# A weight ring of three slots instead of four, and half an expert chunk fetched early into the freed memory

## The reference, cut to what matters

```python
proj = h @ w_in[l]                       # first block: 1024 x 15368
ym = hm @ w_proj_m[l]; ya = ha @ w_proj_a[l]
x = x + gate[:, None] * (y @ w_out[l])
# second block: w_in, w_out again, and then
xs = jax.vmap(lambda hb, ib: hb[ib])(h, idx)
a = jnp.einsum('becd,edf->becf', xs, w_gate)
u = jnp.einsum('becd,edf->becf', xs, w_up)
y = jnp.einsum('becf,efd->becd', jax.nn.silu(a) * u, w_down) * gate[..., None]
```

## Time and profile before

| | |
|---|---|
| median of 3 runs | 1555.35 us (1554.5 to 1555.72) |
| profiled execution, its own time | 1554.04 us |
| span of that execution | 1552.2 us |
| TensorE busy | 1198.4 us (77%) |
| VectorE busy | 614.4 us (40%) |
| ScalarE busy | 425.8 us (27%) |
| HBM read | 548.36 MB |
| rate of the transfers, slices 17 to 39 of 40 | 390 to 432 GB/s |
| dense loads at L520 | 93 of 1 MiB, 5.4 us from issue to landing in the median |

### The profile page before, as it was taken

One profiled execution on the slowest core, in us unless ns is written; L12 is line 12 of the kernel. 1 busy time (PEld: TensorE's weight loads), 2 busy tenths in 40 slices (PEclk: granted clock), 3 DMA queues, 4 the chain that ended last, 5 costly groups with the idle time before them and its releaser, 6 DMA issues.

```text
span 1552.2 us, 18204 instructions
## 1 busy us (share of the span) xinstructions
PE 1198.4 (77%) x7368; PEld 696.7 (45%) x7368; DVE 614.4 (40%) x1041; ACT 425.8 (27%) x644; POOL 36.9 (2%) x62
## 2 busy tenths in 40 slices
PE   7999999999999999976666665665655665665665
PEld 5888977887887899721111111111111111111112
DVE  3786789889777876511011011011011011110111
ACT  3665357786554674300000000000000000000001
POOL 0000000010001000000000000000000000000000
PEclk9999999999999999988777787787878877777788
DMA  9876877687756666999999999999999999999996
GB/s 362 284 263 216 308 245 246 231 307 235 273 183 209 215 220 245 390 432 430 430 432 430 430 431 432 430 432 432 432 429 431 432 430 431 431 430 430 432 432 276
DMA packets 78323, 550.62 MB, mean 355 GB/s; under 512 B 5032, under 2 KB 5320, under 8 KB 61856
## 3 DMA queue, kind: packets, MB, share of 16 engines
q1 hardware_dynamic: 75168, 541.08, 86.2%
q0 software_dynamic: 2784, 8.08, 1.7%
q10 hardware_dynamic: 288, 0.30, 0.1%
HBM read 548.36 MB, written 1.61 MB: 354 GB/s over the span
## 4 chain that ended last, share of the span: by engine, by line
PE 43%; DMA 36%; DVE 12%; ACT 4%; issue 3%; SPq 0%; DVEq 0%; ACTq 0%; POOL 0%
PE ps L610 41%; DMA b<-in_w_down 34%; DVE b L1535 6%; ACT b L1171 3%; PE ps L614 3%; DVE b L1552 2%; DVE b L2265 1%; ACT b L1173 1%; DVE b L2206 1%; DMA b<-in_w_in 1%; DMA b<-in_w_ada 1%; DVE b L2212 1%; DVE b L1545 0%; ACT L1171 0%; DVE b L1566 0%
## 5 line engine op out<-in xcount | busy, mean ns | idle before, releaser
L610 PE MATMUL ps<-b,b 128*32 128x512 f32 (+7 forms) x6922 | 1130.3, 541 | 300.0 <-DMA b<-in_w_up 117.3
L610 PEld LDWEIGHTS ps<-b,b 128*32 128x32 f32 (+2 forms) x6922 | 640.9, 159 | 750.5 <-issue 456.5
L1171 ACT ACTIVATE b<-ps 128x512 f32<-128x512 f32 (+3 forms) x165 | 92.2, 559 | 868.7 <-PE ps L610 560.7
L1535 DVE TENSOR_TENSOR b<-b,b 128x1024 fp32r<-128x1024 f32 (+5 forms) x254 | 277.1, 1091 | 98.1 <-ACT b L1171 78.9
L1171 ACT ACTIVATE b<-b 128x1024 fp32r<-128x1024 f32 (+6 forms) x219 | 219.1, 1001 | 213.9 <-PE ps L610 161.2
L2255 DVE TENSOR_TENSOR b<-b,ps 128x512 f32<-128x512 f32 x16 | 11.0, 687 | 395.6 <-issue 382.3
L2265 DVE TENSOR_TENSOR b<-b,ps 128x1024 f32<-128x1024 f32 x28 | 34.2, 1222 | 304.3 <-PE ps L610 304.3
L614 PE MATMUL ps<-b,b 128*128 128x128 f32 (+1 forms) x360 | 69.7, 322 | 38.4 <-DVE b L1566 23.5
L614 PEld LDWEIGHTS ps<-b,b 128*128 128x128 f32 (+1 forms) x360 | 45.8, 168 | 88.9 <-DVE b L1566 36.4
L1552 DVE SCALAR_TENSOR_TENSOR b<-b,b,b 128x512 f32<-128x512 f32 (+3 forms) x50 | 63.2, 1263 | 4.3 <-ACT b L1171 0.5
L1535 DVE TENSOR_TENSOR b<-ps,b 128x512 f32<-128x512 f32 (+8 forms) x69 | 37.6, 545 | 26.5 <-PE ps L610 14.9
(11 more groups left out here) (59 smaller groups left out, 201.0 us busy)
## 6 DMA issues: line engine op xcount, KB each, us to landing
b<-in_w_up SPq DMA_DIRECT2D x30, 4096.0 KB, 43.2
b<-in_w_gate SPq DMA_DIRECT2D x29, 4096.0 KB, 43.0
b<-in_w_down SPq DMA_DIRECT2D x29, 4096.0 KB, 38.5
b<-in_w_in SPq DMA_DIRECT2D x73, 1024.0 KB, 5.6
b<-in_w_ada SPq DMA_DIRECT2D x28, 1024.0 KB, 5.5
b<-in_w_gate SPq DMA_DIRECT2D x6, 2048.0 KB, 9.0
b<-in_w_down SPq DMA_DIRECT2D x5, 2048.0 KB, 13.0
b<-in_w_ada SPq DMA_DIRECT2D x16, 512.0 KB, 11.4
```

The lines of the kernel that those rows point to most:

```text
L610: return e.matmul(o, lhsT, rhs, start=start, stop=stop, skip_group_check=True)
L1171: e.activation(o, i, f, bias=bias, scale=scale).then_inc(mark[0], 1)
L1535: e.tensor_tensor(o, a, b, op).then_inc(mark[0], 1)
```

## The change

`RING` becomes 3, so that load i goes to slot i % 3 and waits for the load three places before it. The memory of the fourth slot (24 to 32 KB of the ring's area) is the upper half of the place of chunk 7. This half (1 MiB, columns 2048 to 4095 of the chunk) is now fetched right behind chunk 0, before load 92. The lower half, which lies in slot 2, is fetched where the whole chunk was. The waits for chunk 7 count both halves. The sizes and the number of bytes stay, and there is one transfer more.

```diff
--- before.py
+++ after.py
@@ -167,7 +167,7 @@
     ADA_STEP[_step] = [ADA_STEP[_step], NADA_PE + _a] if _step in ADA_STEP else NADA_PE + _a
 ADA_AT = {step: a if isinstance(a, list) else [a] for step, a in ADA_STEP.items()}
 ADA_SUM = {(13, 0): "R3", (17, 0): "R2", (26, 0): "R4"}
-RING = 4
+RING = 3
 LOADS = []
 
 
@@ -268,6 +268,8 @@
 
 E_PAIR_FREE = (5, 9, 11, 12, 14)
 
+IN_HALVES = E_ORDER.index("ring2")
+
 SCRATCH = 1024
 
 
@@ -476,7 +478,7 @@
         def expert_weight(n):
 
             if n < E_FIRST:
-                return EW[n], (S(f"ew{n}"), 16) if n < NCH else (S(f"ada0_{n % 2}_0"), 48)
+                return EW[n], (S(f"ew{n}"), 32 if n == IN_HALVES else 16) if n < NCH else (S(f"ada0_{n % 2}_0"), 48)
             m, g = (n - E_FIRST) // 2, n % 2
             return EP[m % E_PAIRS][:, g * 4096:(g + 1) * 4096], (S(f"ew{m % E_PAIRS}"), 16 * (m // E_PAIRS + 2))
 
@@ -531,6 +533,11 @@
                 ada0(1, k)
                 if k == 0:
                     ring_load(2)
+            def half_load(n, h):
+                o, (landed_, _) = expert_weight(n)
+                hs = slice(h * 2048, (h + 1) * 2048)
+                e.dma_start(o[:, hs], chunk_src(n)[:, hs]).then_inc(landed_, 16)
+
             def expert_load(n):
                 o, (landed_, _) = expert_weight(n)
                 e.dma_start(o, chunk_src(n)).then_inc(landed_, 16)
@@ -538,6 +545,7 @@
             for i in range(3, len(LOADS) - 1):
                 if LOADS[i] == ("w", SLACK):
                     expert_load(0)
+                    half_load(IN_HALVES, 1)
                 if LOADS[i] == ("w", CONTEXT_DONE):
 
                     e.wait_ge(S("v_x"), 2 * NT)
@@ -560,7 +568,7 @@
             e.wait_ge(S("v_ry"), 1)
             expert_load(6)
             e.wait_ge(S("v_lo"), NHALF - 4)
-            expert_load(7)
+            half_load(IN_HALVES, 0)
             e.wait_ge(S("v_lo"), NHALF)
             expert_load(8)
             e.wait_ge(*full("WP0b"))
@@ -1137,7 +1145,7 @@
 
 
             def last_part(q):
-                e.wait_ge(S(f"ew{E_PAIRS + q}"), 32)
+                e.wait_ge(S(f"ew{E_PAIRS + q}"), 48 if E_PAIRS + q == IN_HALVES else 32)
                 for b in (2 * (q % 2), 2 * (q % 2) + 1):
                     ins = down_last(w, 3, b, q // 2)
                 ins.then_inc(S("p_use"), 1)
```

## The result

The changed kernel took a median of **1574.55 us** (1572.18 to 1574.99, four runs), the kernel before 1555.53 us (1554.5 to 1559.75, four runs): a ratio of **1.012**, 95% interval 1.0104 to 1.0135. The forecast was 1562.0, and slower: the direction was right, and the delay was 19.0 us where the prediction's terms add up to 6.8. The profiled execution took 1572.18 us.

A forecast was written before the change was run, and what follows sets the result against it. It took the experts as bound by their bytes and the dense stages by TensorE. Span 1552.2 + 3.9 + 2.9 = 1559.0, own time 1560.8, median 1.3 above, say 1562.0; range 1554.5 to 1567.

The forecast's parts named there:

- Method: Dense-weight ring: shift each load's issue by one place, then see what time each consumer had in hand.
- Term A: Start, loads 6 and 7 up to the gate products: 3.9 us later, bounds 0 and 4.5.
- 62 to 300 us: Dense stages where TensorE is full: late loads cost 0, bounds 0 and some 6 us.
- Term B: Dense stages from 300 to 366 us, lateness from load 69 on: +2.9 us, bounds 0.8 and 7.3.
- The clock: Sign of being wrong: granted clock under 1.00 from 62 to 300 us, after TensorE's longer wait near 62; no size given.
- 366 us to the end: Rest of the dense stages: three slots still cover a landing of 5 us, no load short of time, 0.
- Term C: Early half at the hand-over, 624 to 658 us: nothing behind it starts sooner, 0, bounds -1.3 and 0.
- rival 1: Ring hides the late loads and the early half's bytes come off the expert stream: 1552.9, not slower; chance 0.19.
- Rival 3: Shortages at the start, to 300 us and from 300 to 366 us add up: 14.8 us, 1570; chance 0.12.
- the remainders' lead: Dense stages: `lo` runs three halves ahead of TensorE, so lateness first uses up 2 x 2.7 us of ready products.

The follow-up runs named there:

- experiment 4: Kernel before with its four slots, but loads 0 to 11 in three slots only: 1561.06 us, ratio 1.0028.
- experiment 6: Kernel before with its four slots, but loads 12 to 59 in three slots; chunk 7 whole at its old place: 1560.2 us, ratio 1.0025.
- experiment 5: Kernel before with its four slots, but loads 60 to 83 in three slots; chunk 7 whole at its old place: 1566.32 us, ratio 1.0058.
- experiment 9: Changed kernel, three slots, with the last 4 modulation loads one dense load later in the issue order: 1568.47 us, ratio 1.0085 to the kernel before.
- experiment 1: Changed kernel's three slots without the early half; chunk 7 fetched whole at its old place: 1574.7 us, ratio 1.0126 to the kernel before.
- experiment 3: Changed kernel, but loads 0 to 11 may take all four slots; early half kept: 1567.84 us, ratio 1.0083 to the kernel before.
- experiment 8: Kernel before, but three slots from load 84 on and the early half fetched as in the change: 1555.99 us, ratio 1.0009.
- experiment 2: Kernel before, four slots, with the upper half of chunk 7 set to zero instead of fetched, 1 MiB less: 1555.99 us, ratio 1.0006.
- experiment 11: Kernel before, four slots, with the last four modulation loads one dense load later: 1554.6 us, ratio 0.9994.
- experiment 12: Kernel before, four slots, with the last eight modulation loads one dense load later: 1553.37 us, ratio 0.9989.
- experiment 10: Changed kernel, three slots, with the last 8 modulation loads one dense load later: 1568.38 us, ratio 1.0079 to the kernel before.
- experiment 7: Changed kernel, three slots, with all 20 modulation loads that VectorE reads one dense load later: 1593.92 us, ratio 1.0239 to the kernel before.

## Why the prediction was right in direction and wrong in size

**Method** (load i goes out where load i + 1 did): it holds for the first load that is late, in both places: load 6 out at 47.83 instead of 47.72 forecast, and ScalarE at load 69 3.9 us worse instead of 3.76. What it can't give is the second and third load behind it, as it shifts everything by the times of a trace in which hardly anything was late.

**Term A, 3.9 us:** 3.7 in the profile, 4.4 by the ratio of experiment 4 (0.28%, interval 2.2 to 6.7 us). The profile alone wouldn't show it, as starts with four slots lie up to 3.0 us apart (last section). The size held, by luck; the path was load 6, hi(10), hi(11), two reads and hi(12), where the prediction had load 7's 9.3 us. Load 7 took 7.9.

**62 to 300 us, 0:** 1.7 in the profile, and 3.9 us by the ratio of experiment 6 (interval 1.9 to 5.9; the upper bound was 6). So this term was not 0. Where the prediction read some ten loads up to 2.3 us late, ScalarE waited 14 times, up to 4.9 us; of these 38.7 us nearly all were covered.

**Term B, 2.9 us, is the step that failed.** It measured 12.6 in the profile, beyond its upper bound of 7.3, and 9.0 us by the ratio of experiment 5 by itself (0.58%, interval 5.9 to 12.1), so it didn't need the start's lateness. Its first step was near: load 69 made half 89 2.6 us later (7.4 to 10.0), where it had 2.1. Three parts of its working are wrong:

1. "It now waits for lo(93), 342.2, lands 4.9 us on": the landings were 6.96 and 7.83 us, as each goes out 1.3 to 1.6 us behind a modulation load. With three slots the one waits for VectorE's read of a modulation load, the other for a `lo`, and VectorE ends the two 1.3 to 1.6 us apart. With four slots they were further apart, and the dense loads landed in 5.11 and 4.99. The figure stood in the trace of before: loads 73 and 76, which went out at the moments to which the method moves loads 72 and 75, took 7.07 and 8.10. With 8.10 in place of 4.9, load 75 lands at 350.3, 3.9 us behind the old hi(96) and not 0.8; at the start the prediction did take the rows of the same moment. Its estimate of 4.4 us for 1 MiB, by the Trainium skill, DMA: Bandwidth & Descriptors (Anatomy of one DMA), rests on a fit that the page gives for transfers issued by GpSimd. SP's ring loads took 4.8 to 7.8 us in this stretch.
2. "Half 93 ... with 0.6 in hand": the lead was subtracted anew at each load. VectorE is busy for 56.9 of 66 us there, so a lead once used up doesn't come back before the next late load. TensorE's lateness went from 5.4 at half 80 to 7.4 at half 87, 10.0 at 89, 12.2 at 93, 14.4 at 97 and 18.0 at 100, and none was given back. The first 2.0 us came ahead of load 69, where the prediction had nothing; in experiment 5, which came in on time, they were 0.2.
3. The loop was not followed: a late landing makes `hi` and `lo` late, and `lo` is the release for the load three places on. The chain shows it: 330.25, 341.79, 354.92.

How the 12.6 divide between 1, 2 and 3 is open. What is shown: the clock has 1.7 in the profiled execution, and the order of the last 4 modulation loads accounts for 5.4 by the ratios of the change and experiment 9 (1.012 and 1.0085), 6.1 by their medians. A ring whose slots are released by halves, which would break the loop and leave the bytes as they are, was not tried.

**The clock** was named as what the prediction leaves out, in the first stretch. It came there: behind a wait of 2.06 us that ended at 58.20 it was 0.50 from 59.3 for 3.4 us, where it was 1.00 before.
```profile
60.00:61.00 1.00, 1.00 (x4) 0.81 (x3) 0.85 (x3) 0.82 (x3) 0.00 (x0) 0.50 0.58 88
```
It cost nothing in this execution, as the gate products still waited 0.44 us for VectorE. It came again in the third stretch, where it cost 1.7 us.

**366 us to the end, 0,** and **Term C, 0:** both held in the changed kernel. The lateness stays at 17.8 to 18.0 us from half 100 to chunk 12 (in the profiles of experiments 1, 3 and 5 TensorE lost another 1.0 to 1.6 us by 400 us), experiment 8 has the time of before within its interval, and the stream from chunk 12's issue to the end of the span is 896.0 to 896.9 us in all fourteen traces. Of rival 1 (the bytes count) experiments 1 and 2 leave nothing.

**The parts add up:** experiments 4, 6 and 5 give 1.0028, 1.0025 and 1.0058, together 1.1%; the change 1.2%. Rival 3 (the shortages add up, 1570, at 0.12) came nearest, and that they add up is borne out; its 7.3 us for the second place was too small as well, as it doesn't have the loop either. It was held down by "the remainders' lead", which covers the first stretch but not the third, where VectorE and ScalarE are nearly as full as TensorE.

## What to carry to other kernels

In this kernel a slot less cost most where loads held for different lengths share the ring and the engines that release them are nearly full. In such a place follow the loop landing, release, next issue over several turns, and not single loads; and when a load's issue moves to another's moment, take that one's time to landing with it. A lead is an account: subtract it once, and let it grow again only by what the feeding engines have free. Before paying for bytes fetched early, see what gates the first transfer of the stream behind: here it was a release, and 1 MiB more or less ahead of it moved nothing.

## What was not expected of the hardware

- The same wait of TensorE, 2.19 us, was followed by 3.4 us at 1.2 GHz in the changed kernel and by none in experiment 5. The kernel before and that of experiment 2 run the same instructions up to 600 us, and both have a wait of 1.95 us, ended at 472.56 and at 477.08: the clock stayed at 1.00 in the one and was 0.50 for 3.4 us in the other, which made TensorE 1.6 us later. So one profiled execution can hold such a dip and another not.
- The start differs between executions, with equal loads. With four slots the gate products began at 62.26 (before), 63.26, 64.04, 64.43, 64.67, 64.72 and 65.25 us (experiments 5, 8, 6, 11, 12 and 2), and at 61.29, without a wait of TensorE there, in experiment 3; with three at 65.94, 66.12, 65.91, 68.57, 68.80 and 69.03 (the change, experiments 1, 10, 7, 4 and 9). The kernel before's own profile, from which Term A was worked out, was one of the best starts with four slots; the profile of experiment 2, with four slots too, sent chunk 12 out 6.1 us later than it.
- Loads 72 and 75 took 5.11 and 4.99 us with nothing out close ahead of them, and 6.96 and 7.83 when another transfer of 1 MiB had gone out 1.3 to 1.6 us ahead on the same queue, while that one took 4.8 to 4.9. The kernel before has it as well: of its ring loads of 70 to 410 us the 14 that went out under 2 us behind another took 6.6 to 9.5. It isn't the only reason for a long landing: in experiment 9 the load out at 326.73 took 7.2 with nothing out for 7.6 us ahead of it.
